# Two long convolutions of a two-block model in fp32: taps of two tiles in turn, layer norm statistics in four column tiles and per token, z projections moved behind later tiles

## The reference

```python
def layer_norm(x, g, b):                      # over the 2048 channels of a token
    mu = mean(x); var = mean(square(x - mu))
    return (x - mu) * rsqrt(var + 1e-6) * g + b

def causal_depthwise_conv(x, w):              # out[t, c] = sum_k w[k, c] * x[t - 30 + k, c]
    ...

def conformer_conv_mixer(h, w_in, conv_w, conv_b, ln_g, ln_b, w_out):
    val, glu_gate, z = split(h @ w_in, 3)     # h: 256 x 1024, w_in: 1024 x 6144
    u = val * sigmoid(glu_gate)
    u = causal_depthwise_conv(u, conv_w) + conv_b
    u = silu(layer_norm(u, ln_g, ln_b))
    return (u * silu(z)) @ w_out              # w_out: 2048 x 1024

def first_block(x, ...):                      # mixers: long conv, attention, short conv, long conv
    for kind in (0, 1, 2, 0):
        x = x + mixer[kind](rms_norm(x, g))
```

## Time and profile before

| | |
|---|---|
| time, median of 3 runs (range) | 1524.62 us (1522.92 to 1525.06) |
| the profiled execution's own time | 1521.88 us |
| its span, first to last instruction | 1520.1 us |
| TensorE busy | 1491.1 us (98%), 10457 matmul records |
| VectorE busy | 1048.9 us (69%) |
| ScalarE busy | 828.2 us (54%) |
| GpSimd busy | 502.8 us (33%) |
| mean granted TensorE clock | 0.998 of 2.4 GHz |

### The profile page before, as it was taken

One profiled execution on the slowest core, in us unless ns is written; L12 is line 12 of the kernel. 1 busy time (PEld: TensorE's weight loads), 2 busy tenths in 40 slices (PEclk: granted clock), 3 DMA queues, 4 the chain that ended last, 5 costly groups with the idle time before them and its releaser, 6 DMA issues.

```text
span 1520.1 us, 27235 instructions
## 1 busy us (share of the span) xinstructions
PE 1491.1 (98%) x10457; PEld 1387.7 (91%) x10457; DVE 1048.9 (69%) x2144; ACT 828.2 (54%) x1525; POOL 502.8 (33%) x464
## 2 busy tenths in 40 slices
PE   7999999999999999999999999999999999999998
PEld 6888899998899999999988888989888878999998
DVE  5899966555787786666599997656247667775522
ACT  4676666545666544444456676545346656554442
POOL 1777642433333200000057785055421112000043
PEclk9999999999999999999999999999999999999999
DMA  7554365666744567866444445564853123576553
GB/s 198 144 152 139 129 196 160 224 173 149 138 139 157 153 191 206 208 182 194 140 139 139 139 139 166 181 160 117 216 154 99 56 88 136 167 194 194 161 171 113
DMA packets 325013, 239.54 MB, mean 158 GB/s; under 512 B 18017, under 2 KB 309235, under 8 KB 324884
## 3 DMA queue, kind: packets, MB, share of 16 engines
q1 hardware_dynamic: 312808, 228.70, 52.1%
q10 hardware_dynamic: 12076, 9.09, 2.6%
HBM read 236.02 MB, written 1.75 MB: 156 GB/s over the span
## 4 chain that ended last, share of the span: by engine, by line
PE 79%; DVE 14%; ACT 3%; issue 1%; DMA 1%; POOL 1%; DVEq 0%; SPq 0%; ACTq 0%; POOLq 0%
PE bank L744 16%; PE bank L746 7%; PE bank L747 7%; PE bank L748 7%; PE bank L795 3%; DVE bank L1069 3%; PE bank L797 3%; PE bank L796 3%; PE bank L1586 3%; PE bank L1588 3%; PE bank L1587 3%; DVE wlo L380 2%; PE bank L1213 2%; PE bank L758 2%; PE bank L818 1%
## 5 line engine op out<-in xcount | busy, mean ns | idle before, releaser
L380 POOL TENSOR_TENSOR wlo<-ring,whi 128x1024 fp32r<-128x1024 f32 (+1 forms) x106 | 255.4, 2416 | 853.9 <-ACT whi L371 853.9
L371 ACT CAST whi<-ring 128x1024 fp32r<-128x1024 f32 (+1 forms) x340 | 341.1, 1020 | 230.4 <-PE bank L748 78.6
L380 DVE TENSOR_TENSOR wlo<-ring,whi 128x1024 fp32r<-128x1024 f32 (+2 forms) x234 | 292.6, 1259 | 182.3 <-ACT whi L371 180.9
L744 PE MATMUL bank<-sqb,ring 128*128 128x256 f32 x1504 | 330.3, 380 | 1.1 <-DVE sqb L646 1.1
L744 PEld LDWEIGHTS bank<-sqb,ring 128*128 128x128 f32 x1504 | 285.7, 190 | 40.8 <-issue 1.3
L746 PE MATMUL bank<-xh,whi 128*128 128x256 f32 x928 | 265.1, 286 | 2.7 <-DVE xl L668 2.7
L747 PE MATMUL bank<-xl,whi 128*128 128x256 f32 x928 | 263.9, 284 | 0.0
L748 PE MATMUL bank<-xh,wlo 128*128 128x256 f32 x928 | 263.9, 284 | 0.0
L1006 POOL TENSOR_TENSOR scratch<-scratch 128x256 f32<-128x256 f32 x288 | 200.1, 731 | 110.9 <-ACT scratch L951 100.2
L1069 DVE SCALAR_TENSOR_TENSOR bank<-scratch,convw,bank 128x256 f32<-128x256 f32 x576 | 231.1, 483 | 0.0
L746 PEld LDWEIGHTS bank<-xh,whi 128*128 128x128 f32 x928 | 179.2, 193 | 5.8 <-issue 2.9
(11 more groups left out here) (303 smaller groups left out, 2849.6 us busy)
## 6 DMA issues: line engine op xcount, KB each, us to landing
ring<-in_a_w_in_dram SPq DMA_DIRECT2D x64, 512.0 KB, 5.1
ring<-in_b_w_in_dram SPq DMA_DIRECT2D x32, 1024.0 KB, 6.0
ring<-in_c_w_in_dram SPq DMA_DIRECT2D x64, 512.0 KB, 5.4
ring<-in_w_in_dram SPq DMA_DIRECT2D x26, 1024.0 KB, 5.3
ring<-in_w_ffn_in_dram SPq DMA_DIRECT2D x44, 512.0 KB, 5.2
ring<-in_a_w_in_dram SPq DMA_DIRECT2D x16, 1024.0 KB, 5.1
ring<-in_a_w_out_dram SPq DMA_DIRECT2D x16, 1024.0 KB, 5.6
ring<-in_w_ffn_out_dram SPq DMA_DIRECT2D x16, 704.0 KB, 4.5
```

What stands on the lines that cost most here:

```text
L371: nc.scalar.copy(piece(whi, h)[:, :, 0:n], src).then_inc(hi_done, 1)
L380: engine.tensor_tensor(piece(wlo, h)[:, :, 0:n], src, piece(whi, h)[:, :, 0:n].bitcast(F32), ALU.subtract).then_inc(done, 1)
L744: mm = nc.tensor.matmul(o, halves[h][1][:, k, :], sqb[:, k, :], start=(k == 0), stop=(k == KD - 1))
```

## The change

It does five things in `conf_*`, in both long convolutions:

1. VectorE's taps: tiles 0, 1, 2 and 15 go alone as before; 3 to 14 go in pairs, a tap of the one and a tap of the other in turn, each tile with one accumulator of its own, so that `join` is one instruction per tile. `up` has 4 slots. `gated` stands 2 to 3 tiles ahead.
2. ScalarE's order: `sigmoid(c+2)` stands in tile c (from tile 3 on), `square(c-2)` instead of `square(c-3)`; the ring of squares has 3 buffers instead of 4, and `square(c)` waits for the sums of the pair two before.
3. The sums: `pair_sums(q)` gives tiles 2q and 2q+1 four matmuls with a 128x32 matrix (one column of ones), each to its own 32 partitions of bank 7: four column tiles. They stand behind tiles 8, 10, 12 and 14 and between the last z units.
4. The statistics: ScalarE copies bank 7, TensorE transposes it (`stats_turned`), so that a token's sums are numbers on its partition; VectorE works on 128x2 numbers, makes diagonal matrices of them, and TensorE spreads them to all partitions again with two matmuls (`spread`), inside z(6). VectorE centres and scales two tiles in one instruction (128x512).
5. The z units: z(0) to z(3) stand behind tiles 8, 12, 14 and 15 (before 3, 7, 11 and 15); `conf_z(0)` before `sigmoid(9)`, `conf_z(1)` before `sigmoid(13)`, `conf_z(2)` in tile 14. The output units' splits stand at tiles 10 and 15.

```diff
+        Z_BESIDE = {6: 5, 11: 6, 15: 7}
+        OUT_BESIDE = {10: 0, 15: 1}
+        TILE_GROUPS = [(0,), (1,), (2,)] + [(c, c + 1) for c in range(3, KE - 1, 2)] + [(KE - 1,)]
+        SIGMOIDS = {0: (1,), 1: (2,), 2: (3, 4)} | {c: (c + 2,) for c in range(3, KE - 2)}
+        SQUARES = {3: (0,), 4: (1, 2)} | {c: (c - 2,) for c in range(5, KE)}
+        SUMS = {8: (0, 1), 10: (2,), 12: (3,), 14: (4,)}
+        Z_BEHIND = {8: 0, 12: 1, 14: 2, KE - 1: 3}
 # conf_act
             def sigmoid(c):
-                if c % 4 == 0 and c:
-                    conf_z(act, n, c // 4 - 1)
+                if c in (9, 13):
+                    conf_z(act, n, (c - 9) // 4)
...
             def square(c):
                 act.wait_ge(conv_done, j * KE + c + 1)
-                wait(act, sqm_done, j * KE + c - 3)
+                wait(act, sqm_done, j * (KE // 2) + (c - 3) // 2 + 1 if c >= 3 else 0)
...
                     if i == TAPS_POOL // 3:
-                        if c + 1 < KE:
-                            sigmoid(c + 1)
-                        else:
-                            conf_z(act, n, 3)
-                    if i == 2 * TAPS_POOL // 3 and c >= 3:
-                        square(c - 3)
+                        for s in SIGMOIDS.get(c, ())[0:1]:
+                            sigmoid(s)
+                        if c == KE - 2:
+                            conf_z(act, n, 2)
+                    if i == 2 * TAPS_POOL // 3:
+                        for s in SIGMOIDS.get(c, ())[1:]:
+                            sigmoid(s)
+                        for s in SQUARES.get(c, ()):
+                            square(s)
...
-            for c in range(KE - 3, KE):
+            for i in range(3, 5):
+                conf_z(act, n, i)
+            for c in range(KE - 2, KE):
                 square(c)
-            conf_z(act, n, 4)
+            nc.scalar.activation(l_warm, eps, ACT.Sqrt)
+            act.wait_ge(sqm_done, (j + 1) * (KE // 2))
+            nc.scalar.copy(x_sums, bank[7][:, 0:S]).then_inc(mean_done, 1)
             act.wait_ge(var_done, j + 1)
-            nc.scalar.activation(std[:, 0:S], std[:, 0:S], ACT.Sqrt, bias=eps).then_inc(lstd_done, 1)
+            nc.scalar.activation(l_var, l_var, ACT.Sqrt, bias=eps).then_inc(lstd_done, 1)
 # conf_dve, the taps of a pair
+                for i in range(TAPS_DVE * len(cs)):
+                    a = i % 2
+                    k, c = (i // 2, cs[a]) if pair else (i, cs[0])
+                    if pair and i == 12:
+                        join(gi - 1)
+                    ...
+                    if pair and i == 16 and cs[0] + 3 < KE:
+                        gated(cs[0] + 2)
+                    if pair and i == 34:
+                        gated(cs[0] + 3 if cs[0] + 3 < KE else cs[0] + 2)
 # conf_dve, the statistics
+            chain(dve, nc.vector.tensor_reduce(l_sums, sums, AX, ALU.add))
+            chain(dve, nc.vector.tensor_scalar(l_negm, l_sums[:, :, 0], -1.0 / E, None, ALU.mult))
+            chain(dve, nc.vector.tensor_tensor(l_msq, l_negm, l_negm, ALU.mult))
+            nc.vector.scalar_tensor_tensor(l_var, l_sums[:, :, 1], 1.0 / E, l_msq, ALU.mult, ALU.subtract).then_inc(var_done, 1)
+            diagonal(0, l_negm)
+            dve.wait_ge(lstd_done, j + 1)
+            chain(dve, nc.vector.reciprocal(l_rstd, l_var))
+            diagonal(1, l_rstd)
 # conf_pe
+            def pair_sums(q):
+                pe.wait_ge(conv_done, j * KE + 2 * q + 2)
+                pe.wait_ge(sqd_done, j * KE + 2 * q + 2)
+                srcs = [yb[:, 2 * q, :], yb[:, 2 * q + 1, :], csq[:, 2 * q % 3, :], csq[:, (2 * q + 1) % 3, :]]
+                for i, src in enumerate(srcs):
+                    mm = nc.tensor.matmul(bank[7][32 * i:32 * i + 32, 0:S], one_column, src, start=(q == 0), stop=(q == KE // 2 - 1))
+                mm.then_inc(sqm_done, 1)
...
-                if c % 4 == 3:
-                    i = c // 4
-                    if i:
-                        pe.wait_ge(sz_done, j * 8 + i)
+                if c in Z_BEHIND:
+                    i = Z_BEHIND[c]
+                    wait(pe, sz_done, j * 8 + i if i else 0)
                     proj_T(pe, *n["z"][i], at=z_bank(n, i))
...
+            pair_sums(5)
             proj_T(pe, *n["z"][4])
...
+            proj_T(pe, *n["z"][5], at_k={KD - 1: lambda: pair_sums(6)})
+            pair_sums(7)
+            proj_T(pe, *n["z"][6], at_k={1: stats_turned, 3: lambda: spread(0), 6: lambda: spread(1)})
+            proj_T(pe, *n["z"][7])
```

More of the change, by code:

```diff
@@ L1010, in conf_pool @@
             for c in range(KE):
-                if c in AHEAD_BESIDE:
-                    lo_pool_to(pool, ahead(n["z"][AHEAD_BESIDE[c]][1]))
                 if c in OUT_BESIDE:
-                    lo_pool_to(pool, ahead(n["out"][OUT_BESIDE[c]][2]))
+                    lo_pool_to(pool, last(n["out"][OUT_BESIDE[c]][2]))
                 pool.wait_ge(act_done, j * KE + c + 1)
@@ L1021, in conf_dve @@
             j = n["j"]
-            for r in range(3):
+            for r in range(4):
                 nc.vector.memset(up[:, r, 0:TAPS - 1], 0.0).then_inc(pad_done, 1)
-            dve.wait_ge(pad_done, 3 * j + 3)
+            dve.wait_ge(pad_done, 4 * j + 4)
             if j == 0:
@@ new lines, in conf_dve, with join @@
+            ended = {}
+            def join(gi):
+                cs = TILE_GROUPS[gi]
+                for a, c in enumerate(cs):
+                    done = raw_done if c < 3 else conv_done
+                    dve.wait_ge(pool_sum, j * KE + c + 1)
+                    dve.wait_ge(step, ended[gi][a])
+                    if len(cs) == 2:
+                        nc.vector.tensor_tensor(yb[:, c, :], acc[gi % 2][:, a, :], accp[:, c % 2, 0, :], ALU.add).then_inc(done, 1)
+                        continue
+                    chain(dve, nc.vector.tensor_tensor(yb[:, c, :], acc[gi % 2][:, 0, :], accp[:, c % 2, 0, :], ALU.add))
+                    dve.wait_ge(step, ended[gi][1])
+                    nc.vector.tensor_tensor(yb[:, c, :], acc[gi % 2][:, 1, :], yb[:, c, :], ALU.add).then_inc(done, 1)
@@ new lines, in conf_dve @@
+                ended[gi] = prev
+                if gi in (1, 2):
+                    if gi == 2:
+                        gated(4)
+                    join(gi - 1)
+                if gi == 2:
+                    dve.wait_ge(shift_done, j + 1)
+                    shifted(0)
+                    shifted(1)
+            join(len(TILE_GROUPS) - 1)
+            dve.wait_ge(stat_tr, j + 1)
+            sums = bank[6][:, 0:S].rearrange("p (b s e r) -> p b s e r", b=TB, s=2, e=2)[:, :, :, :, 0]
@@ new lines, in conf_dve @@
+            for q in range(2):
+                centre(q)
+            dve.wait_ge(stat_spread, 2 * j + 2)
+            for q in range(KE // 2 + 2):
+                if q + 2 < KE // 2:
+                    centre(q + 2)
+                if q < KE // 2:
+                    dve.wait_ge(dc_done, j * (KE // 2) + q + 1)
+                    nc.vector.tensor_tensor(yb[:, 2 * q:2 * q + 2, :], yb[:, 2 * q:2 * q + 2, :], both(2), ALU.mult).then_inc(dn_done, 1)
+                for c in (2 * q - 1, 2 * q):
+                    if c in OUT_BESIDE:
+                        lo_dve_to(dve, last(n["out"][OUT_BESIDE[c]][2]))
+                for c in (2 * q - 3, 2 * q - 2):
+                    if 0 <= c < KE:
+                        y_low(dve, n["y0"] + c, y_hi[:, c, :], y_lo[:, c, :])
```

180 lines of the change are left out of this document (75 added, 105 removed).

## The result

The changed kernel takes 1550.72 us (median of 4 runs, 1549.36 to 1552.46), the kernel before 1524.84 (4 runs, 1522.92 to 1525.37): a ratio of 1.0173, with a 95% interval of 1.0155 to 1.019. It is slower, by 25.9 us; I had forecast 1540.3 with a range of 1524 to 1552. The sign and the main mechanism were right. The sum was 10 us short, and 1550.7 lies outside the 1530 to 1546 that I had given my own forecast; only the wider range, stretched for the slow rivals, holds it.

A forecast was written before the change was run, and what follows sets the result against it. TensorE was taken as the bound, VectorE and GpSimd close behind; (2.7 + 3.8) + (2.7 + 3.5) + 3.0 = +15.7 us on 1521.88, with the median 2.74 above, gave 1540.3 us, range 1524 to 1552 (its own 1530 to 1546).

The forecast's parts named there:

- the slow rivals: Only two column tiles share the array, 1547 us, chance 0.12; clock stays low through z(3), 1551 us, chance 0.06.
- sums removed and added: TensorE, per convolution: 64 records removed, -13.8 us; eight groups in four column tiles at 0.65 us added, +5.2 us.
- waits for squares: ScalarE's squares come late, so sums of pairs or a projection wait: +1.2 us per convolution, bounds 0.5 and 3.
- transposes, spreads and their wait: Statistics on TensorE: two transposes and two matmuls, +1.1 us; waiting for VectorE ahead of spread(0), +0.8 us.
- z(3)'s wait: TensorE waits for ScalarE's eviction of z(2), which shares bank 2: +8.2 us per convolution, bounds 7.5 and 9.
- the clock behind it: TensorE's clock after each 8.2 us gap costs 1.5 us, +3.0 for both; bounds 0 and 6.9.
- output's start: TensorE waits for the splits of the first two output units: +3.8 us in the first convolution, +3.5 in the second.
- VectorE's margin at tiles 7 and 8: gated(c-2) is done when TensorE comes to tile c; margin smallest there, about 1 to 3 us.
- the 5 to 6 that I gave as a sign: Sign at the output projection: the first L798 starts 5 to 6 us later than before in both layers.
- What before lost at its eighth half unit: Output projection of the kernel before: its eighth half unit began 1.4 us late, counted as -1.4 in the first convolution.
- my rival of a clock that stays low: Clock falls and stays low through z(3): +10.8, 1551 us, chance 0.06.
- The rival of a faster kernel: TensorE does not wait at z(3), as z(2) is out when tile 15's projection ends: 1521 us or 1515, chance 0.13.

The follow-up runs named there:

- experiment 5: Changed kernel, from the second pair on all four sums of a group go to the same 32 partitions, one behind the other: 1565.69 us, 1.0271.
- experiment 1: Changed kernel with z(2)'s eviction on ScalarE moved to tile 13, ahead of the gate of tile 15: 1529.64 us, 1.0033.
- Experiment 2: Changed kernel with z(5)'s eviction on ScalarE moved ahead of the first scaling of the normalisation: 1550.41 us.
- experiment 12: Changed kernel, z(2) and z(5) evicted early, output splits 0, 1, 2 at tiles 0, 11, 13, four unread matmuls filling the start: 1520.37 us, 0.9974.
- experiment 4: Changed kernel with 18 more matmuls nobody reads between tile 15's projection and z(3), in each long convolution: 1542.91 us, 1.0123.
- experiment 8: Changed kernel, z(2) and z(5) evicted early, splits of output units 0 and 1 at tiles 0 and 11: 1529.45 us, 1.0031.

## Why the prediction was right, and where it was short

The traces account for the long convolutions as follows, us against the kernel before (the profiled spans differ by 28.5, of which 2.7 are the two starts told above). From first projection to last output matmul the traces give 12.7 and 14.0, the 1.7 us of the first projection left aside; the rest of the program is 0.9 us shorter.

| step | predicted, each | first | second |
|---|---|---|---|
| sums removed and added | -13.8 + 5.2 | -13.8 + 5.8 | same |
| waits for squares | +1.2 | +2.0 | +2.0 |
| transposes, spreads and their wait | +1.1 + 0.8 | +1.1 + 0.4 | same |
| z(3)'s wait | +8.2 | +8.3 | +8.3 |
| the clock behind it | +1.5 | +3.05 | +2.4 |
| output's start | +3.8, +3.5 | +5.7 | +7.5 |
| sum | +8.0, +7.7 | +12.6 | +13.7 |

*Sums*: the mechanism held, shown by experiment 5. The group's price was 0.07 us low: from the two-tile rows I read the entry and the exit together as 0.21, and four tiles pay 0.29 beside the 0.43 of their records.

*Squares*: pair 0 waited 0.69 and pair 1 1.57 us, less 0.3 that before had. Tile 5's square waited for TensorE 5.5 us in the first convolution, where the issue of DMAs had held ScalarE for 7 us just ahead of tile 5, and 7.1 in the second, where nothing did; I had 10. The pair behind it still came late.

*z(3)*: the path (sigmoid of tile 15, taps, table load, eviction) was as written, to 0.1 us, and experiment 1 shows that it is the cause of 21.1 of the 25.9 us. VectorE's margin at tiles 7 and 8 held, too: no projection waits for its gates.

*The clock*: the mechanism was right and the size too small. I read 1.5 us off sixteen transposes; the unit behind the gap lost 3.05 and 2.4. The bound of 6.9 for a whole unit at 1.2 GHz wasn't reached: the clock was back for the last 4 of z(3)'s 10 us. And I took from the earlier trace rows that the kernel before shows no fall. Its trace has one in the second block, where TensorE runs matmuls of 30 columns and has no wait right ahead of it; a digit that stands for 38 us hides it, since 9 means 90% or more:

```profile
1044.00:1046.00 2.00, 2.00 (x12) 1.94 (x12) 0.00 (x0) 0.00 (x0) 0.00 (x0) 0.50 0.69 237
```

There matmuls of 256 columns start 0.21 us apart (`L747` at 1046.09, `L748` at 1046.30), against 0.12 once the clock is back, so the price of a record at the lower level could have been read ahead.

*The start of the output*: this is the step that failed in its working. The prediction said "z(7) ends 15.7 after it" (z(6)'s start) and took waits of 2.4 and 2.8 us for the splits. z(7) ended 21.3 after it, because it waits 3.9 us for z(5)'s eviction and runs 1.8 us longer at the lower clock; I had not looked at who frees the bank of the last units, only at the one shared by z(2) and z(3). So the first `L798` came 13.0 and 12.1 us later in its convolution than before, the start of the program apart, and not the 5 to 6 that I gave as a sign. Experiment 2 shows that the omission isn't what made the time wrong: without that wait unit 0 waits 2.7 (predicted 2.4) and unit 1 3.4 (2.8), and the time stays. The error is in the chain of the normalisation: from the first scaling to unit 1's copies on ScalarE I had 18.6 us, and it is 20.0. In the second convolution GpSimd's low part of unit 1 was ready 23.3 behind the first scaling, not 21.1, and the lower clock behind the wait for it took another 1.7. What before lost at its eighth half unit fell away as I had counted: no wait follows unit 1's in the first convolution.

Together the terms are short by 2.4 (clock), 1.2 (groups), 1.6 (squares) and 5.9 (output), less 0.8 for the wait ahead of the first spread, which was 0.4 each too high: 10.3 of the 10.4 us between 1540.3 and 1550.7. That the total fell near my rival of a clock that stays low (1551) is chance; that rival's mechanism isn't what happened.

The rival of a faster kernel hung on one point, whether z(2) is out in time. Experiment 1 put it so, and the kernel was still 4.7 us slower than before, not 3.7 faster: the chain behind the statistics takes what the sums give. Only with three splits moved forward in that chain and the start filled was the kernel faster than before (experiment 12). The pairs of taps and the per-token statistics were not taken out by themselves in any run, so what they give alone is not measured.

## What to carry to other kernels

When units of work are moved later on one engine, walk every buffer they use to the instruction on another engine that frees it, and ask what that instruction is queued behind; here one eviction behind the wrong sigmoid cost 21 us, and a place where ScalarE idled anyway stood a tile earlier. Removing a wait shows as time only if the next thing in the chain isn't late by as much: measure the distance from the event that starts the chain (here the first scaling) to the work that is held, and if it stays the same with and without the wait (22.5 and 22.2 us), the chain is the bound. A gap on TensorE should be counted with the slower work behind it. And when a last variant beats the kernel before, ask which of its edits would have helped that one too.

## What the runs showed of the hardware that I had not expected

- Work that nobody reads made the kernel faster: 7.8 us of matmuls in each 8.3 us gap took 7.8 us off the time; 5.2 of these are z(3) behind it, which took 7.17 us and not 10.12 and 9.44.
- The clock's price behind nearly equal gaps varies from trace to trace: behind 8.3 us the same unit took 8.75 to 10.12 us in the traces; behind 3.6 to 3.9 us, z(7) took 8.86 in the changed kernel and 10.01 in the second convolution of experiment 4.
- Behind a start gap of 1.1 to 1.5 us the first projection took 7.14 to 7.15 us, behind 1.8 to 2.3 it took 8.55 to 8.83. The runs of before, and of experiment 8, fall in two groups some 2.6 us apart, the quicker one with the short start; filling the gap took 2.6 us off experiment 8's median.
- Four column tiles of 256 columns cost 0.72 us between two units of projection, the same eight records in one tile 2.0.
